# Three narrow column blocks of a three-layer kernel: weights packed by partition and split four tiles at a time, and another order of the first loads

## The reference

```python
# layer 0: the last 16 columns of w_in are the low-rank gate
proj = h @ w_in                                    # 2048 x (1024+1024+2048+2048+16)
q, k, v, gate, gk_low = jnp.split(proj, [...], axis=-1)
gk = gk_low @ w_gk2 + b_gk
# layer 1: 64 columns for the rotary key
proj = h @ w_in                                    # 512 + 512 + 64 + 2048 columns
c_q, c_kv, k_rope, gate = jnp.split(proj, [...], axis=-1)
# layer 2: 24 gate columns and 16 delta-net columns, in two places of w_in
```

## Time and profile before

| | |
|---|---|
| time, median of 3 runs | 2406.88 us (2406.26 to 2407.22) |
| the profiled execution: its own time | 2404.23 us |
| the profiled execution: span, first to last instruction | 2402.5 us |
| TensorE busy / VectorE busy / ScalarE busy | 97% / 61% / 54% of the span |
| mean granted TensorE clock | 0.991 |
| DMA | 408.94 MB, mean 170 GB/s, 247404 packets, of which 29713 under 512 B |

### The profile page before, as it was taken

One profiled execution on the slowest core, in us unless ns is written; L12 is line 12 of the kernel. 1 busy time (PEld: TensorE's weight loads), 2 busy tenths in 40 slices (PEclk: granted clock), 3 DMA queues, 4 the chain that ended last, 5 costly groups with the idle time before them and its releaser, 6 DMA issues.

```text
span 2402.5 us, 33358 instructions
## 1 busy us (share of the span) xinstructions
PE 2337.5 (97%) x12514; PEld 1985.3 (83%) x12514; DVE 1468.0 (61%) x2567; ACT 1296.1 (54%) x2393; POOL 18.3 (1%) x38
## 2 busy tenths in 40 slices
PE   8999999899999899999999999999999999999998
PEld 7877788788888899778787887888888888888887
DVE  4554565675665655886676566656666666665554
ACT  5645455665565544775555545555555555554444
POOL 1000000000000000000000000000000000000000
PEclk9999999999999999999999999999999999999999
DMA  6555566456435465656453225655666666665554
GB/s 213 158 167 149 165 203 194 139 158 183 124 123 192 142 184 165 186 158 197 143 166 118 83 80 176 220 185 180 186 188 189 186 191 185 188 205 190 191 190 167
DMA packets 247404, 408.94 MB, mean 170 GB/s; under 512 B 29713, under 2 KB 62529, under 8 KB 246865
## 3 DMA queue, kind: packets, MB, share of 16 engines
q1 hardware_dynamic: 243392, 393.20, 54.7%
q0 software_dynamic: 3136, 10.26, 1.2%
q10 hardware_dynamic: 720, 3.42, 0.4%
HBM read 400.53 MB, written 6.29 MB: 169 GB/s over the span
## 4 chain that ended last, share of the span: by engine, by line
PE 89%; DVE 5%; ACT 4%; issue 1%; DMA 0%; SPq 0%; DVEq 0%; ACTq 0%
PE banks L361 50%; PE banks L335 14%; PE banks L355 9%; PE banks L337 7%; DVE weights_low L306 2%; PE banks L644 1%; ACT weights_high L303 1%; PE banks L804 1%; PE banks L2221 1%; PE banks L2210 1%; PE banks L1681 1%; PE banks L815 0%; DMA weight_ring<-in_w_gla_in 0%; PE banks L1102 0%; PE banks L2283 0%
## 5 line engine op out<-in xcount | busy, mean ns | idle before, releaser
L306 DVE TENSOR_TENSOR weights_low<-weight_ring,weights_high 128x512 fp32r<-128x512 f32 (+3 forms) x1512 | 1007.1, 675 | 841.7 <-ACT weights_high L303 812.5
L303 ACT CAST weights_high<-weight_ring 128x512 fp32r<-128x512 f32 (+3 forms) x1512 | 910.2, 609 | 1002.8 <-PE banks L361 637.8
L361 PE MATMUL banks<-weights_high,hidden_T 128*128 128x512 f32 x3008 | 865.9, 400 | 10.8 <-DVE weights_low L306 9.6
L361 PEld LDWEIGHTS banks<-weights_high,hidden_T 128*128 128x128 f32 x3008 | 557.0, 189 | 135.3 <-issue 12.8
L361 PE MATMUL banks<-weights_low,hidden_T 128*128 128x512 f32 x1504 | 466.7, 391 | 0.0
L335 PE MATMUL banks<-hidden_T,weights_high 128*128 128x512 f32 x1408 | 385.1, 394 | 0.6 <-DVE residual L2829 0.6
L361 PEld LDWEIGHTS banks<-weights_low,hidden_T 128*128 128x128 f32 x1504 | 283.3, 188 | 61.6
L335 PEld LDWEIGHTS banks<-hidden_T,weights_high 128*128 128x128 f32 x1408 | 240.4, 189 | 32.9 <-DVE residual L2829 0.8
L337 PEld LDWEIGHTS banks<-hidden_T,weights_low 128*128 128x128 f32 x1408 | 216.5, 189 | 30.3
L337 PE MATMUL banks<-hidden_T,weights_low 128*128 128x256 f32 x1408 | 224.4, 281 | 0.0
L355 PE MATMUL banks<-hidden_T,weights_high 128*128 128x256 f32 (+3 forms) x1120 | 185.3, 286 | 6.9 <-DVE weights_low L306 5.9
(11 more groups left out here) (400 smaller groups left out, 1737.2 us busy)
## 6 DMA issues: line engine op xcount, KB each, us to landing
weight_ring<-in_w_in SPq DMA_DIRECT2D x168, 512.0 KB, 3.6
weight_ring<-in_w_gla_in SPq DMA_DIRECT2D x96, 512.0 KB, 3.8
weight_ring<-in_w_gate SPq DMA_DIRECT2D x88, 512.0 KB, 3.7
weight_ring<-in_w_ffn_up SPq DMA_DIRECT2D x88, 512.0 KB, 3.6
weight_ring<-in_w_down SPq DMA_DIRECT2D x88, 512.0 KB, 3.8
weight_ring<-in_w_mla_in SPq DMA_DIRECT2D x49, 512.0 KB, 3.6
weight_ring<-in_w_gla_out SPq DMA_DIRECT2D x32, 512.0 KB, 4.2
weight_ring<-in_w_mla_out SPq DMA_DIRECT2D x32, 512.0 KB, 4.3
```

The costliest lines, as they stand in the source:

```text
L303: nc.scalar.copy(hi, raw).then_inc(high_ready, 1)
L306: nc.vector.tensor_tensor(lo, raw, hi.bitcast(F32), ALU.subtract).then_inc(low_ready, 1)
L361: last = pe.matmul(ps[:, b + t, 0:width], a[:, t * P:(t + 1) * P], w, start=(k == 0 and n_th == 0), stop=(k == kt - 1 and n_th == 2))
```

## The change

The three narrow blocks are laid out anew by the host, each as an array of its own: 128 rows (one for each partition) that hold all 16 k tiles one behind the other. Such a block is then loaded with one DMA of 128 rows of 1, 4 and 2.5 KB. It is split four k tiles at a time (`PACK`): the chunk now has 4 "tiles" of 64, 256 and 160 columns. TensorE does the same 48 matmuls for each block, now 12 after each wait. The side steps are renumbered to the smaller number of splits. At the start ACT's queue loads the gain, the identity alone, and the low-rank block; the three masks move to POOL's load. ACT does one `activation` on a single column as soon as the constants have landed, and ACT and DVE do all remaining transposed groups of X right after the first four splits.

```diff
+        def packed_columns(w, width):
+            def piece(slot, k, n):
+                return slot.rearrange("p a n -> p (a n)")[:, 0:KD * width], w
+            return Gathered(1, piece), KD // PACK, 0, 0, PACK * width, hidden, PACKED
...
+            def load_first(self, eng):
+                w = self.chunks[0][0]
+                for n in range(w.pieces):
+                    eng.dma_start(*w.piece(ring[:, self.use0 % SLOTS, :, :], 0, n)).then_inc(landed[self.use0 % SLOTS], 16)
...
+                elif turned == PACKED:
+                    each = width // PACK
+                    for j in range(PACK):
+                        ahi, alo = acts(PACK * k + j)
+                        cs = slice(j * each, (j + 1) * each)
+                        for w, a, n_th in ((hi, ahi, 0), (hi, alo, 1), (lo, ahi, 2)):
+                            last = pe.matmul(ps[0:each, b, 0:S], w[:, cs], a, start=(k == 0 and j == 0 and n_th == 0),
+                                             stop=(k == kt - 1 and j == PACK - 1 and n_th == 2))
...
-        const_head = sum(cols[name][1] for name in ("ident", "upto", "after", "ones"))
+        const_head = cols["ident"][1]
...
-        prod_gla = Product([(A["w_gla_in"], KD, G_LOW, 0, GLA_RANK, hidden, True)]
+        prod_gla = Product([packed_columns(A["w_low"], GLA_RANK)]
...
-                        if k == (0, 0, 4, 8)[j]:
+                        if k == (0, 0, 1, 2)[j]:
...
-                    pe.wait_ge(low_out, turn0.first + k // 2 + 1)
+                    pe.wait_ge(low_out, turn0.first + 2 * k + 2)
...
+        Q_SLOT = KD - PARTS
+        def gla_side_scalar(gos):
-            pace = Pace()
-            for n in (0, 1, 2, 3, 6, 7):
-                yield from pace.to(n)
-                next(turns)
+            pace = Pace(Q_SLOT)
...
-                            (A["w_mla_in"], KD, 2 * W, 0, ROPE, hidden, True)])
+                            packed_columns(A["w_krope"], ROPE)])
...
-            for n, norm in enumerate((norm_q, norm_kv)):
-                yield from pace.to(16 + 16 * n + 2)
-                prod_lat.wait_chunk(nc.scalar, n)
-                yield from pace.run(norm.scalar_steps(), 4)
-            yield from pace.to(50)
+            yield from pace.to(18)
+            prod_lat.wait_chunk(nc.scalar, 0)
+            yield from pace.run(norm_q.scalar_steps(), 4)
+            yield from pace.to(32)
+            prod_lat.wait_chunk(nc.scalar, 1)
+            yield from pace.run(norm_kv.scalar_steps(), 3)
             mla_tables_scalar()
-            yield from pace.to(51)
+            yield from pace.to(39)
...
-            for n, norm in enumerate((norm_q, norm_kv)):
-                yield from pace.to(16 + 16 * n + 4)
-                yield from pace.run(norm.vector_steps(), 3)
+            yield from pace.to(20)
+            yield from pace.run(norm_q.vector_steps(), 2)
             yield from pace.run(mla_tables_vector())
+            yield from pace.to(33)
+            yield from pace.run(norm_kv.vector_steps(), 3)
...
-        prod_nab = Product([(gate_columns(), KD, 0, 0, NAB, hidden, True)])
+        prod_nab = Product([packed_columns(A["w_nab"], NAB)])
...
             for j in range(D // W):
                 sp.dma_start(*x_block(j)).then_inc(s_x[j], 16)
-            for p in (prod_gla, prod_gla_out, prod_lat, ...
+            prod_gla.load(sp, 1)
+            for p in (prod_gla_out, prod_lat, ...
...
-            pool.wait_ge(low_ready, KD)
+            pool.wait_ge(low_ready, prod_gla.chunks[0][1] + 2)
...
+            act.dma_start(small["l0_pre"][:, :], A["small"]["l0_pre"]).then_inc(s_first, 16)
             act.dma_start(const[:, 0:const_head], A["const"][:, 0:const_head]).then_inc(s_first, 16)
-            act.dma_start(small["l0_pre"][:, :], A["small"]["l0_pre"]).then_inc(s_first, 16)
+            prod_gla.load_first(act)
             act.wait_ge(s_first, 32)
+            Sc(act.activation(stat[:, 60:61], ident[:, 0:1], ACT.Copy))
             for _ in range(2):
                 next(turns)
             prod_gla.prime(act)
-            prod_gla.run(act, range(13), gla_evict, prod_gla_out, gla_side_scalar(turns, gos))
+            for _ in turns:
+                pass
+            prod_gla.run(act, range(13), gla_evict, prod_gla_out, gla_side_scalar(gos))
```

More of the change, by code:

```diff
@@ L27 @@
 PARTS = 4
+PACK = 4
 W = 512
@@ L172, in program, with __init__ @@
         class Pace:
-            def __init__(self):
-                self.slot = 0
+            def __init__(self, slot=0):
+                self.slot = slot
             def to(self, slot):
@@ L253, in over, with load @@
                     body(self.rounds - 1)
-            def load(self, sp):
+            def load_first(self, eng):
+                w = self.chunks[0][0]
+                for n in range(w.pieces):
+                    eng.dma_start(*w.piece(ring[:, self.use0 % SLOTS, :, :], 0, n)).then_inc(landed[self.use0 % SLOTS], 16)
+            def load(self, sp, first=0):
                 def body(i):
-                    u = self.use0
-                    for chunk in self.chunks:
+                    u = self.use0 + first
+                    for chunk in self.chunks[first:]:
                         w, kt, col0, step, width, _, _ = chunk
@@ L1234, in gla_gate, with gla_side_vector @@
             v.sem_inc(gn_out, 1)
-        def gla_side_vector(turns, gos):
+        def gla_side_vector(gos):
             v = nc.vector
-            pace = Pace()
-            for n in (0, 1, 2, 3, 6, 7):
-                yield from pace.to(n)
-                next(turns)
+            pace = Pace(Q_SLOT)
             yield from pace.to(SQUARES_AT + 4)
@@ L3077, in _ @@
             prod_gla.prime(v)
-            prod_gla.run(v, after=prod_gla_out, side=gla_side_vector(turns, gos))
+            for _ in turns:
+                pass
+            prod_gla.run(v, after=prod_gla_out, side=gla_side_vector(gos))
             post_vector(prod_gla_out, 0, prod_lat, gla_out_side(gos, lambda: gla_gate(3)))
@@ L3206, with columns @@
     }
+    gla_low, mla_rope, nsa_gates = (2 * GLA_QK + 2 * GLA_V, GLA_RANK), (2 * MLA_RANK, ROPE), (NSA_H * HD + 6 * NSA_KV * HD, 3 * NSA_H)
+    dn_gates = (nsa_gates[0] + 3 * NSA_H + 4 * DN_H * HD, 2 * DN_H)
+    def columns(w, *parts):
+        return np.concatenate([w[:, at:at + n] for at, n in parts], 1).reshape(KD, P, -1).transpose(1, 0, 2).reshape(P, -1)
+    arrays.update({"w_low": columns(a["l0_gla_w_in"], gla_low), "w_krope": columns(a["l1_mla_w_in"], mla_rope),
+                   "w_nab": columns(a["w_in_2"][0], nsa_gates, dn_gates)})
     arrays.update({"small_" + k: v for k, v in small.items()})
```

19 lines of the change are left out of this document (6 added, 13 removed).

## The result

The changed kernel takes 2394.3 us (median of 5 runs, 2393.83 to 2395.66), the kernel before beside it 2406.81 us (5 runs, 2405.16 to 2407.22): a ratio of 0.995 [0.9937, 0.9963], 12.5 us by the medians and 8.9 to 15.2 us by the interval. The median is 3.5 us less than the forecast of 2397.8, and 1.0 under the low end of its range; the forecast gain of 9.1 us lies inside the interval, near its lower end. The profiled execution took 2394.95 us, with a span of 2393.2; the forecast made for that execution, before its offset was added, was 2395.1.

A forecast was written before the change was run, and what follows sets the result against it. TensorE, busy 97% of the span, bounds the kernel, so only holes at three narrow blocks can go: 4.0 + 3.7 + 1.4 = 9.1 us, giving 2395.1 for the profiled execution and 2397.8 against the median. Range: 2396.3 less 1, up to 2402.

The forecast's parts named there:

- First transposes: At the start, the first transposes of X move from 6.38 to about 5.65 us.
- if the identity lands by 5: Condition at the start for the table load to cost nothing; otherwise some 0.7 us of it shows.
- Low-rank block: Load at the start, 128 KB in rows of 1 KB: must land by 8.3 us, 6.8 is near.
- First product matmul: Start of the 16-column block: at 9.5 us, not 12.03.
- query chunk: Work after the 16-column block: starts at 18.8 us with clock loss, not 22.79; gain 4.0, bounds 2.4 and 5.2.
- 64-column block: Narrow block before the gate product: 48 matmuls in 5.6 us instead of 9.34, gain 3.7, bounds 3.1 to 3.9.
- 40-column block: Later narrow block: 5.6 us instead of 6.97, gain 1.4, bounds 1.0 to 1.5.
- C: At the start, X or the identity lands late, first product matmul at 11: gain 2.5 there, time 2399.3; chance 0.09.
- D: At the gate product, ACT is late and a wait of 1.5 us appears: time 2399.3; chance 0.07.
- A: TensorE stays at 1.2 GHz through the whole first block: start loses 1.7 us, time 2403.5; chance 0.07.
- B: Half clock goes on into the query chunk, each us of it costing one more: up to 2426 us; chance 0.02.
- the last sentence of the sum: Carries 2395.1 us, forecast from the profiled execution, to 2397.8 against the median, since that execution ran 2.65 under it.

The follow-up runs named there:

- the two blocks alone: The kernel before with only the 64- and 40-column blocks packed and split four k tiles at a time, start as before: 2400.38 us, ratio 0.9979.
- the 128-row product: The kernel before with its low-rank product contracting over 128 rows, 112 of them zeros, instead of 16: 2404.35 us, ratio 0.9989.
- four versions: Edits of the changed kernel: no early activation 2394.39 us; constants in old order 2394.45; low-rank block on SP's queue 2395.02; warm-up with earlier turns 2394.7.

## Why the prediction was right and wrong

**The steps.** First transposes: 5.65 forecast, 5.52 measured. What came last was not the block of X, though, but the identity, landed at 5.48 after 4.27 us; that was named as a condition ("if the identity lands by 5"), and missed by half a us without harm, since the table load was done at 3.45. Low-rank block: landed at 8.1, where 6.8 was near and 8.3 needed; it just held. First product matmul: 9.5 forecast, 9.62. The first tile took 1.86 us instead of 1.4, at the slow distance, then the forecast pace held: DVE's last group ended at 16.9 (16.4 forecast), query chunk at 18.38 (17.8 without a loss by the clock, 18.8 with the 1.0 taken). Gain 4.41 for 4.0. POOL at 18.41, for "about 18"; no wait at its constants.

64-column block: 5.45 us for 5.6, gain 3.9 for 3.7, at the upper end for the reason given (48 matmuls 0.34 us apart by threes). The packed split costs 0.41 us on ACT and 0.43 on DVE, not 0.35. ACT's eviction, squares and gate tiles came as laid out, and tile 0 of the gate product was ready at 477.01, 3.0 us into the block (3.2 forecast). 40-column block: 5.63 for 5.6, gain 1.3 for 1.4. Waits at the old line 355: 1.6 + 0.4 = 2.0, for "about 2".

Sum by blocks: 9.6 for 9.1; against the profiled execution 2395.1 was forecast and 2394.95 measured. That the two agree to 0.15 us is luck: half a microsecond more at the blocks is offset by what the clock takes on the way, and a second trace of the changed kernel took 2394.47.

**The rivals.** C and D did not come. A and B did not come as put: no half clock in the narrow block beyond its first tile or in the query chunk. The first 16 transposes (3.73 us) and part of that first tile (1.86 us) ran at the slow distance, and full speed came by 10.8 us, where A had the half clock until 24.5. The Trainium skill's "TensorE: Matmul & The Clock Gate", Part 1, makes the slow state the default that activity ends, and this trace agrees. A was nearer than it looks: in one of the four traces of the kernel before the slow distance lasts until 17.4 us. A stretch of half clock did appear where none was before, at 51.5 us, and cost 1.5; a list of rivals should have held "somewhere else" too.

**The step that failed** is the last sentence of the sum: "it ran 2.65 us under the median of 2406.88, and against that median it is 2397.8". It carries over the offset of one execution as if it belonged to both kernels. The changed kernel has no such offset: its two profiled executions lie 0.65 above and 0.75 under the medians of their five runs. The profiled execution of the kernel before was of the faster of two kinds. Four traces show them: 2404.23, 2403.82 and 2403.95 with an early full speed and no half clock behind the low-rank product, 2408.77 with a slow start (1.0 us) and 6.8 us of half clock there (3.1 us). The medians of 2406.2 to 2406.9 lie between. The changed kernel's ten runs lie between 2393.83 and 2396.12, and both its traces have a short stretch, 3.4 us, at that place. The range inherited the error: its low end, 2396.3 less 1, is the upper bound of the gains against the median. Against the profiled execution the same bound is 2404.23 - 10.6 = 2393.6, which is under the measured 2394.3, and both figures should have been inside: an execution 2.65 us off the median, with the three runs 1.0 apart, had itself said that the spread was larger than the 1 us taken.

**What is shown and what is not.** Shown: 9.3 of the 12.5 us are the three blocks, less what the clock takes and gives on the way; the shared split removes the holes, not the layout; two executions of the same program differ by 4.9 us with the same waits, of which 3.1 are a half-clock stretch and 1.0 is TensorE at the slow distance at the start. Shown within some 2 us: that the parts add. Not shown: that there are 3 us beyond the blocks at all. All 84 timed executions of the kernel before have a median of 2406.5 us and the ten of the changed kernel 2394.7, which leaves 2.5 us over the traces' 9.3, and the interval of the result reaches down to 8.9. Shown in part: that the clock at the start makes up what is over. The trace of the two blocks alone, with the slow start and the stretch, is near its median, and the 128-row product took 2.3 us from the kernel before. But 51 of 79 executions of the kernel before have the same mean granted clock as the fast profiled ones, 0.991, and their median is still 2406.0. Since the slow distance before the first change is not counted in it, that mean does not tell the kinds apart, and how many untraced executions are of the slower kind was not seen. Open: why the stretch comes in some executions of one program and not in others, and why, once it is gone from the changed kernel, another appears elsewhere.

## What to carry to other kernels

Where TensorE's piece per split is small against what ACT and DVE do between splits, put several pieces under one split and one wait; the number of buffers then covers several times the work, and a plain re-layout of the same block does nothing for that. Sum a change against the profiled execution, and before carrying it to a median ask what that execution lacks; with an offset larger than the spread of the runs, keep both figures in the range, and trace one program several times before calling a difference of a few us explained. A gain of 1 or 2 us at the start of a long kernel that is bound by TensorE can be taken back by a stretch at half clock (here 1.5 us), so measure it at the end. To see whether the clock is full early in a trace, look at the distance of equal matmuls, not at the granted clock.

## What the runs showed of the hardware that was not expected

- One program without any change ran from 2401.55 to 2409.29 us, and two of its traces, 4.8 us apart, have the same waits. Stretches at half clock of 3.4, 6.8 or 10.2 us came at some seven places of a trace, and traces of kernels that differ within the first 60 us alone differ in the stretches at 51, 589, 790 to 801 and 1111 us. The cost of 3.4 us more of half clock was 1.5 us at 51 us, 1.1 at 801 and nothing that could be seen at 1386.
- A start that was 4.3 us earlier or later in four versions (16.38 to 20.68) left medians 0.6 us apart, of five runs each. In the traces a late start has no stretch near 51 us, but the earliest one kept 1.8 of its 2.0 us to the end.
- The granted clock reads 1.00 from 5 to 10 us of the kernel before and after, while 16 transposes take 3.73 us there and 8 take 1.03 at 11.48: before its first change that column is no evidence of full speed. In the execution of 2408.77 us it reads 1.00 while TensorE is slow until 17.4 us.
- The first load of 8 KB on a queue landed in 2.8 us, the same load behind 256 KB in 5.1. The table load for ACT ran at 2.17 us, as soon as ACT had issued its three DMAs, though the activation behind it waited for the identity until 5.50.
